# Turning the hidden rows of a feed-forward round by VectorE blocks and an exchange through device memory, in place of TensorE transposes

## The chip, the cores and the metric

The kernel runs on one core of one Trainium2 chip. The metric is the time of one execution in microseconds, the median over repeated runs. The unchanged kernel takes 1331.05 us (three runs, 1330.53 to 1331.22).

## What is computed

A first block of two layers (feed-forward, attention and retention mixer, feed-forward, each with a layer norm) is followed by a second block of two mixer layers. There are 256 tokens and a model width of 1024, all in float32. The change touches the four feed-forward stages alone (feed-forward 1 and 2 of both layers):

```
D_FF = ((8 * D_MODEL // 3 + 127) // 128) * 128        # 2816

def swiglu_ffn(x, w_gu, w_down):
    a, u = jnp.split(x @ w_gu, 2, axis=-1)
    return (jax.nn.silu(a) * u) @ w_down

x = layer_norm(DEEPNORM_ALPHA * x + 0.5 * swiglu_ffn(x, ffn1_w_gu[l], ffn1_w_down[l]), ln1_g[l], ln1_b[l])
```

## The kernel before

The program is one list of jobs, `JOBS`, which all engines walk in the same order; each engine takes from a job the part that is its own. The list thus sets the order on every engine's queue. For a feed-forward stage `ffn_jobs` writes it. Semaphore values (`at[...]`) are counted once over the whole list.

**Precision.** Every product of float32 matrices is made of three passes: each operand is split into a high part (ScalarE copies it to the type fp32r) and a low part (VectorE subtracts the high part from the original). TensorE then multiplies high by high, high by low and low by high into the same PSUM bank (`three`, L818 to L820).

**Weights.** Five slots of 1 MB each hold weight units. SyncE (SP) loads a unit, in two halves, as soon as TensorE has given back the slot (L803, after the wait of L785). ScalarE makes `w_hi` (L1141, waits for the DMA), VectorE makes `w_lo` in place of the raw weights (L1317, waits for ScalarE), TensorE waits for `w_lo`. `with_splits` places these split jobs (`hi`, `lo`) in the list, most of a round ahead of their use.

**A feed-forward stage** has 11 rounds of 256 hidden columns. Round `r` is:

- `gu`: for each of the two token tiles `i`, 24 matmuls of 512 columns (gate and up side by side) into PSUM bank 4 + `i`. ScalarE takes the silu of the gate half (L1182), VectorE multiplies it by 0.5 and the up half (L1404), which gives `hidden`, 128 tokens x 256 columns for each tile.
- `ht`: four TensorE transposes of 128x128 (`turn`, L902) put the hidden rows as columns into PSUM bank 6; ScalarE copies the high part to `lat_hi` (L1190), VectorE the low part to `lat_lo` (L1328, from PSUM).
- `down`: for each token tile 12 matmuls of 512 columns with `lat_hi` and `lat_lo` as the weights of the array, added into banks 0 to 3. `down(r)` stands about two rounds behind `gu(r)`.

In between stand jobs that compute the modulation row of the second block, one chunk a round: `modsum` (VectorE, L1415 and L1417, on a chunk that GpSimd's queue loads), `modsplit` (ScalarE L1186, VectorE L1423), `spread` (one TensorE matmul with one column of weights, L946, that sums over the partitions) and `modrow` (VectorE L1428 and L1429). In the list `ht(r-1)` stands behind `gu(r, 0)`, that is behind the first token tile of the next round, with `spread` right behind it.

ScalarE issues no DMA in this kernel: SP issues the weights, GpSimd the parameters.

## Time and profile before

| what | value |
|---|---|
| median of three runs | 1331.05 us (1330.53 to 1331.22) |
| profiled execution, first to last instruction (its span) | 1328.9 us |
| TensorE (PE) busy | 1311.6 us, 99% |
| VectorE (DVE) busy | 1019.8 us, 77% |
| ScalarE (ACT) busy | 675.3 us, 51% |
| GpSimd (POOL) busy | 105.4 us, 8% |
| DMA | 264.92 MB, 199 GB/s over the span |

For the profiled execution the profile gives the span alone; the median lies 2.15 us above it, which is what a run holds ahead of the first and behind the last instruction, plus the difference between executions. Matmuls are pipelined, so that a matmul's busy time overlaps that of the next one: what a matmul costs is read from the start of one to the start of the next, not from its mean.

### The profile page before, as it was taken

Reading aid. Unit: us, or ns where it says so; the run is one execution under the profiler, and the core shown is the slowest. Engines: PE = TensorE matmul, PEld = TensorE weight load, DVE = VectorE, ACT = ScalarE, POOL = GpSimd, SP = SyncE. Lnnn points to the kernel's source line nnn. Section 1 sums busy time; section 2 is a strip of 40 time slices with the busy share of each in tenths; the row PEclk is TensorE's granted clock in tenths of the full one; section 3 lists DMA queues with packets and bytes.
Section 4 is the critical chain, followed back from the end, with each engine's and each line's share of the span. In section 5 each row is a group of like instructions: output and inputs, shape, how many; then the busy total and the mean of one; then the engine's idle time right before and its main releaser. Section 6 shows DMA issues by size and latency. Waiting matters only on the chain.

```text
span 1328.9 us, 18838 instructions
## 1 busy us (share of the span) xinstructions
PE 1311.6 (99%) x7096; PEld 1110.0 (84%) x7096; DVE 1019.8 (77%) x1625; ACT 675.3 (51%) x1069; POOL 105.4 (8%) x153
## 2 busy tenths in 40 slices
PE   9999999999999999999999999999999999999997
PEld 7888888788888888888887888888889998798995
DVE  6677778887777677777787887778676798966986
ACT  6444444644444344444446545444436667457672
POOL 1010100011011001111010011111000000000000
PEclk9999999999999999999999999999999999999999
DMA  8977756527767656776646358777646473463630
GB/s 268 326 232 229 226 187 208 142 96 246 244 228 233 222 185 219 223 236 228 236 161 202 102 173 292 231 253 235 221 142 200 146 237 129 143 214 118 203 128 32
DMA packets 195049, 264.92 MB, mean 199 GB/s; under 512 B 17232, under 2 KB 140240, under 8 KB 194448
## 3 DMA queue, kind: packets, MB, share of 16 engines
q1 hardware_dynamic: 183248, 223.12, 52.1%
q0 software_dynamic: 11712, 40.60, 8.9%
q8 instruction: 57, 0.93, 0.3%
q14 instruction: 32, 0.26, 0.1%
HBM read 262.61 MB, written 1.07 MB: 198 GB/s over the span
## 4 chain that ended last, share of the span: by engine, by line
PE 87%; DVE 7%; DMA 4%; ACT 1%; issue 1%; SPq 0%; DVEq 0%; ACTq 0%
PE ps L818 26%; PE ps L820 26%; PE ps L819 26%; PE ps L902 4%; DVE w_lo L1317 2%; DMA w_raw<-in_ffn_w_gu 2%; PE ps L1049 2%; DMA w_raw<-in_w_in 1%; PE ps L1084 1%; PE ps L1110 1%; DVE few_first L1346 1%; ACT w_hi L1141 1%; DVE y L1345 1%; PE ps L1018 0%; PE ps L1096 0%
## 5 line engine op out<-in xcount | busy, mean ns | idle before, releaser
L1317 DVE TENSOR_TENSOR w_lo<-w_raw,w_hi 128x1024 fp32r<-128x1024 f32 (+2 forms) x420 | 496.9, 1213 | 128.5 <-ACT w_hi L1141 126.5
L1141 ACT ACTIVATE w_hi<-w_raw 128x1024 fp32r<-128x1024 f32 (+2 forms) x420 | 431.0, 1053 | 247.9 <-DMA w_raw<-in_ffn_w_gu 122.0
L818 PE MATMUL ps<-w_hi,col_hi 128*128 128x512 f32 (+2 forms) x1024 | 396.7, 387 | 3.6 <-DVE w_lo L1324 1.4
L820 PE MATMUL ps<-w_hi,col_lo 128*128 128x512 f32 (+2 forms) x1024 | 392.0, 383 | 0.0
L819 PE MATMUL ps<-w_lo,col_hi 128*128 128x512 f32 (+2 forms) x1024 | 391.9, 383 | 0.0
L818 PEld LDWEIGHTS ps<-w_hi,col_hi 128*128 128x128 f32 x1024 | 192.6, 188 | 44.0 <-DVE w_lo L1317 4.3
L820 PEld LDWEIGHTS ps<-w_hi,col_lo 128*128 128x128 f32 x1024 | 192.5, 188 | 38.2
L819 PEld LDWEIGHTS ps<-w_lo,col_hi 128*128 128x128 f32 x1024 | 192.5, 188 | 34.6
L818 PE MATMUL ps<-w_hi,lat_hi 128*128 128x512 f32 (+2 forms) x544 | 208.8, 384 | 0.0
L820 PE MATMUL ps<-w_hi,lat_lo 128*128 128x512 f32 (+2 forms) x544 | 206.5, 380 | 0.0
L819 PE MATMUL ps<-w_lo,lat_hi 128*128 128x512 f32 (+2 forms) x544 | 206.3, 379 | 0.0
L1182 ACT ACTIVATE arena<-ps 128x256 f32<-128x256 f32 x88 | 33.7, 383 | 201.0 <-PE ps L820 200.8
L818 PEld LDWEIGHTS ps<-w_hi,lat_hi 128*128 128x128 f32 x544 | 102.1, 188 | 19.5 <-ACT arena L1218 1.0
L820 PEld LDWEIGHTS ps<-w_hi,lat_lo 128*128 128x128 f32 x544 | 102.1, 188 | 19.0
L819 PEld LDWEIGHTS ps<-w_lo,lat_hi 128*128 128x128 f32 x544 | 102.2, 188 | 18.3
L818 PE MATMUL ps<-col_hi,w_hi 128*128 128x256 f32 x352 | 101.1, 287 | 0.0
L1417 DVE SCALAR_TENSOR_TENSOR mod<-mod,small 128x192 f32<-128x192 f32 x224 | 93.8, 419 | 8.0
L819 PE MATMUL ps<-col_lo,w_hi 128*128 128x256 f32 x352 | 99.6, 283 | 0.0
L820 PE MATMUL ps<-col_hi,w_lo 128*128 128x256 f32 x352 | 99.6, 283 | 0.0
L1404 DVE SCALAR_TENSOR_TENSOR arena<-arena,ps 128x256 f32<-128x256 f32 x88 | 36.6, 416 | 63.4 <-PE ps L902 49.7
L818 PEld LDWEIGHTS ps<-col_hi,w_hi 128*128 128x128 f32 x352 | 67.4, 192 | 1.2 <-issue 0.7
L819 PEld LDWEIGHTS ps<-col_lo,w_hi 128*128 128x128 f32 x352 | 67.4, 192 | 0.2
(148 smaller groups left out, 1172.8 us busy)
## 6 DMA issues: line engine op xcount, KB each, us to landing
w_raw<-in_ffn_w_gu SPq DMA_DIRECT2D x352, 256.0 KB, 4.5
w_raw<-in_w_in SPq DMA_DIRECT2D x108, 512.0 KB, 4.6
w_raw<-in_ffn_w_down SPq DMA_DIRECT2D x88, 512.0 KB, 4.9
mod<-in_w_ada POOLq DMA_DIRECT2D x32, 768.0 KB, 7.6
w_raw<-in_w_out SPq DMA_DIRECT2D x24, 512.0 KB, 4.5
norm_g<-in_ln_g POOLq DMA_DIRECT2D x8, 512.0 KB, 4.2
norm_b<-in_ln_b POOLq DMA_DIRECT2D x8, 512.0 KB, 6.1
w_raw<-in_w_out SPq DMA_DIRECT2D x16, 256.0 KB, 4.5
```

The lines of the kernel that those rows point to most:

```text
L818: pe.matmul(dst, a_hi, b_hi, start=start, stop=False)
L819: pe.matmul(dst, a_hi, b_lo, start=False, stop=False)
L820: return pe.matmul(dst, a_lo, b_hi, start=False, stop=stop)
L902: last = pe.transpose(ps[0:width, 6 + b, c:c + P], src, ident[:, :])
L1049: last = pe.matmul(ps[:, half, q * keys:(q + 1) * keys], a, b, start=True, stop=True)
L1084: last = pe.matmul(ps[64 * half:64 * half + 64, 2 + i, pair * P:(pair + 1) * P], rows2[:, k, v:v + HD], prob_t[:, half, c:c + P], start=k ...
L1110: last = pe.matmul(ps[:, 2 + i, h * HD:(h + 1) * HD], decayed[:, q, half, pair, :], rows1[:, k, VR + h * HD:VR + (h + 1) * HD], start=q < ...
L1141: act.activation(half_of(w_hi[j], n, h), half_of(raw[j], n, h), ACT.Copy).then_inc(hi_ready, 1)
L1182: act.activation(silu_rows[:, nth % 2, :], ps[:, gu_bank(s, r, i), 0:FU], ACT.Silu)\
L1317: tt(half_of(w_lo[j], n, h), half_of(raw[j], n, h), half_of(w_hi[j], n, h).bitcast(F32), ALU.subtract)\
L1404: stt(hidden[:, r % 2, i, :], silu_rows[:, nth % 2, :], 0.5, ps[:, gu_bank(s, r, i), FU:2 * FU], ALU.mult, ALU.mult).then_inc(hidden_done, 1)
L1417: last = stt(ada_sum, ada_w[:, k, :], c_silu[:, k:k + 1], ada_sum, ALU.mult, ALU.add)
```

## The change

In rounds 1 to 8 of each feed-forward stage (32 rounds in all) the job `ht` is gone. Rounds 0, 9 and 10 keep it. Four jobs stand in its place:

- `hturn` (VectorE, right behind `gu(r, 1)`): one block transpose of `hidden`, 128 partitions x 512 elements, each 32x32 block turned within its group of 32 partitions, into `h_blocks` (in `arena`).
- `hstore` (ScalarE's queue, inside `gu(r+1, 0)`): waits for the block turn, then issues one DMA of 256 KB from `h_blocks` to an internal tensor in device memory.
- `hmove` (ScalarE's queue, inside `gu(r+1, 1)`): waits for the landing of that store, then issues four DMAs of 64 KB that read the blocks back, each into a group of 32 partitions of `h_cols`, in runs of 512 bytes.
- `hparts` (behind `gu(r+2, 0)`): waits for the four landings; ScalarE makes `lat_hi` in two copies of 256 elements, VectorE makes `lat_lo` in two subtractions of 256, now from SBUF. `down(r)` waits for these.

`hidden` of round `r+2` no longer waits for the TensorE transposes but for the block turn. The places of the weight splits are unchanged.

```diff
+ROWS_BY_PE = (0, 9, 10)
...
+    by_pe = lambda r: [("ht", s, r)] if r in ROWS_BY_PE else []
+    blocks, stored, moved, parts = (
+        lambda r, kind=kind: [(kind, s, r)] if r >= 0 and r not in ROWS_BY_PE else [] for kind in ("hturn", "hstore", "hmove", "hparts"))
...
+        jobs += gu(1, 0)[:1] + by_pe(0) + gu(1, 0)[1:] + [("params", s)] + gu(1, 1) + blocks(1)
...
-        jobs += gu(r, 0) + [("ht", s, r - 1)]
+        jobs += gu(r, 0)[:1] + stored(r - 1) + gu(r, 0)[1:] + by_pe(r - 1) + parts(r - 2)
...
-        jobs += gu(r, 1)
+        jobs += gu(r, 1)[:1] + moved(r - 1) + gu(r, 1)[1:] + blocks(r)
...
+    jobs += parts(ROUNDS - 2) + down(tail[0], 0) + down(tail[1], 0) + by_pe(ROUNDS - 1) + down(tail[2], 0) + down(tail[3], 0)
...
+        h_blocks = arena[:, 1536:2560].rearrange("p (r b n) -> p r b n", r=2, b=4)
+        h_cols = arena[:, 2560:3584].rearrange("p (r a n) -> p r a n", r=2, a=4)
...
+        h_stage = nc.dram_tensor("hidden_blocks", (2, 4, 32, 4, P), F32, kind="Internal").ap()
...
+        def h_part(tile, q):
+            return tile[:, q:q + 2, :].rearrange("p g (i a t) -> p g i a t", i=TT, a=4)
+
+        h_as_columns = h_cols.rearrange("p r a (i g t) -> p r g i a t", i=TT, g=2)
...
-                    turns_done(("ht", s, r))
+                    if r in ROWS_BY_PE:
+                        turns_done(("ht", s, r))
+                    else:
+                        pe.wait_ge(h_split, at["hparts", (s, r)])
...
+                elif kind == "hstore":
+                    r = job[2]
+                    nth = at["hturn", (s, r)]
+                    act.wait_ge(h_turned, nth)
+                    if nth > 2:
+                        act.wait_ge(h_moved, 64 * (nth - 2))
+                    act.sem_inc(a_marks, 1)
+                    act.dma_start(h_stage[r % 2].rearrange("a f b n -> (a f) b n"), h_blocks[:, r % 2, :, :]).then_inc(h_stored, 16)
+                elif kind == "hmove":
+                    r = job[2]
+                    nth = at["hturn", (s, r)]
+                    act.wait_ge(h_stored, 16 * nth)
+                    if nth > 2:
+                        act.wait_ge(h_split, nth - 2)
+                    act.sem_inc(a_marks, 1)
+                    for b in range(4):
+                        act.dma_start(h_cols[32 * b:32 * b + 32, r % 2, :, :], h_stage[r % 2, :, :, b, :].rearrange("a f n -> f a n"))\
+                            .then_inc(h_moved, 16)
+                elif kind == "hparts":
+                    r = job[2]
+                    q = 2 * (r % 4)
+                    act.wait_ge(h_moved, at["hmove", (s, r)])
+                    if r >= 4:
+                        act.wait_ge(used, NUMBER[s, ("down", r - 4)] + 1)
+                    act.activation(h_part(lat_hi, q)[:, 0], h_as_columns[:, r % 2, 0], ACT.Copy)
+                    act.activation(h_part(lat_hi, q)[:, 1], h_as_columns[:, r % 2, 1], ACT.Copy).then_inc(hi_part, 1)
...
-                    if r >= 2:
+                    if r >= 2 and r - 2 in ROWS_BY_PE:
                         b, n = TURN["ht", s, r - 2][0]
                         dve.wait_ge(turned[b], n + 1)
+                    elif r >= 2:
+                        dve.wait_ge(h_turned, at["hturn", (s, r - 2)])
...
+                elif kind == "hturn":
+                    r = job[2]
+                    dve.wait_ge(hidden_done, at["hidden", (s, r, 1)])
+                    if at["hturn", (s, r)] > 2:
+                        dve.wait_ge(h_stored, 16 * (at["hturn", (s, r)] - 2))
+                    dve.transpose(h_blocks[:, r % 2, :, :].rearrange("p b (c t) -> p b c t", t=32),
+                                  hidden[:, r % 2, :, :].rearrange("p i (g b f) -> p b (i g) f", g=2, b=4)).then_inc(h_turned, 1)
+                elif kind == "hparts":
+                    r = job[2]
+                    q = 2 * (r % 4)
+                    dve.wait_ge(hi_part, at["hi_part", job])
+                    tt(h_part(lat_lo, q)[:, 0], h_as_columns[:, r % 2, 0], h_part(lat_hi, q)[:, 0].bitcast(F32), ALU.subtract)
+                    tt(h_part(lat_lo, q)[:, 1], h_as_columns[:, r % 2, 1], h_part(lat_hi, q)[:, 1].bitcast(F32), ALU.subtract)\
+                        .then_inc(h_split, 1)
```

What moves on TensorE, at the first spread of the first feed-forward stage (names: `w_hi_61` and `w_lo_60` are a weight slot, `arena` holds `hidden`, `col_hi` the turned activations). Before:

```order
L818 MATMUL ps<-w_hi_61,col_hi 128x512
L819 MATMUL ps<-w_lo_60,col_hi 128x512
L820 MATMUL ps<-w_hi_61,col_lo 128x512
L902 MATMUL ps<-ident,arena 128x128 [waits free0,hidden_done]
L902 MATMUL ps<-ident,arena 128x128 x3
L946 MATMUL ps<-ada_both,ones 1x384 [waits free1,mod_lo]
L818 MATMUL ps<-w_hi_58,col_hi 128x512 [waits hidden_done]
```

And in the changed kernel, at the same place (L836 to L838 are the former L818 to L820, L964 the former L946):

```order
L836 MATMUL ps<-w_hi_61,col_hi 128x512
L837 MATMUL ps<-w_lo_60,col_hi 128x512
L838 MATMUL ps<-w_hi_61,col_lo 128x512
L964 MATMUL ps<-ada_both,ones 1x384 [waits free1,mod_lo]
L836 MATMUL ps<-w_hi_58,col_hi 128x512 [waits hidden_done]
```

The four transposes are gone; the spread matmul follows the weights' matmuls directly, and nothing else moved.

What stands on ScalarE's queue in one steady round of the first stage. Before (L1141 are weight splits, L1182 the silu, L1190 the high part of the turned rows, L1186 `modsplit`):

```order
L1182 ACTIVATE arena<-ps 128x256 [waits hidden_done,group_done]
L1190 ACTIVATE lat_hi<-ps 128x512 [waits turned0]
L1141 ACTIVATE w_hi_64<-w_raw_62 128x1024 [waits w_landed40]
L1141 ACTIVATE w_hi_64<-w_raw_62 128x1024 [waits w_landed41]
L1182 ACTIVATE arena<-ps 128x256 [waits hidden_done,w_used]
L1141 ACTIVATE w_hi_52<-w_raw_50 128x2x512 [waits w_landed00]
L1141 ACTIVATE w_hi_52<-w_raw_50 128x2x512 [waits w_landed01]
L1186 ACTIVATE ada_both<-mod 128x192 [waits mod_summed]
L1141 ACTIVATE w_hi_55<-w_raw_53 128x1024 [waits w_landed10]
L1141 ACTIVATE w_hi_55<-w_raw_53 128x1024 [waits w_landed11]
```

In the changed kernel, from the second of the two high-part copies on (L1238; L1203 is the silu, L1162 the weight splits, L1229 the reads of `hmove`, L1207 `modsplit`, L1220 the store of `hstore`):

```order
L1238 ACTIVATE lat_hi<-arena 128x256
L1162 ACTIVATE w_hi_64<-w_raw_62 128x1024 [waits w_landed40]
L1162 ACTIVATE w_hi_64<-w_raw_62 128x1024 [waits w_landed41]
L1229 DMA arena<-hidden_blocks 32x4x128 [waits hidden_blocks_stored,hidden_split]
L1229 DMA arena<-hidden_blocks 32x4x128 x3
L1203 ACTIVATE arena<-ps 128x256 [waits hidden_done,w_used]
L1162 ACTIVATE w_hi_52<-w_raw_50 128x2x512 [waits w_landed00]
L1162 ACTIVATE w_hi_52<-w_raw_50 128x2x512 [waits w_landed01]
L1207 ACTIVATE ada_both<-mod 128x192 [waits mod_summed]
L1162 ACTIVATE w_hi_55<-w_raw_53 128x1024 [waits w_landed10]
L1162 ACTIVATE w_hi_55<-w_raw_53 128x1024 [waits w_landed11]
L1220 DMA hidden_blocks<-arena 128x512 [waits hidden_blocks_turned,hidden_blocks_moved]
```

Five DMA issues a round are new on this queue. Those of `hmove`, with the wait for the store, stand between the splits of one weight unit and the silu of the second token tile; the store stands behind the last pair of weight splits shown and ahead of the silu of the next round's first token tile.

## Rows read from the trace of the kernel before

**Rows 1.** The page: span, busy time by engine.
```profile
span 1328.9 us, 18838 instructions
PE 1311.6 (99%) x7096; PEld 1110.0 (84%) x7096; DVE 1019.8 (77%) x1625; ACT 675.3 (51%) x1069; POOL 105.4 (8%) x153
```

**Rows 2.** Busy time by stretch: us, engines, clock, DMA share, GB/s.
```profile
34.00:51.00 17.00, 17.00 (x79) 14.05 (x78) 7.13 (x13) 7.59 (x10) 0.00 (x0) 1.00 1.03 384
...
585.00:602.00 17.00, 17.00 (x79) 14.10 (x78) 12.56 (x21) 7.50 (x11) 1.92 (x3) 1.00 0.69 224
```

**Rows 3.** Timeline of PE, transposes without a spread: start, us, engine, line.
```profile
523.42 0.39 PE L820 MATMUL ps<-w_hi,col_lo 128*128 128x512 f32 x1
523.65 0.60 PE L902 MATMUL ps<-ident,arena 128*128 128x128 f32 x4
524.00 0.48 PE L818 MATMUL ps<-w_hi,col_hi 128*128 128x512 f32 x1
524.32 0.39 PE L819 MATMUL ps<-w_lo,col_hi 128*128 128x512 f32 x1
```

**Rows 4.** Timeline of PE, transposes with a spread behind them.
```profile
653.42 0.39 PE L820 MATMUL ps<-w_hi,col_lo 128*128 128x512 f32 x1
...
654.49 0.39 PE L819 MATMUL ps<-w_lo,col_hi 128*128 128x512 f32 x1
...
660.17 0.39 PE L820 MATMUL ps<-w_hi,lat_lo 128*128 128x512 f32 x1
```

**Rows 5.** Timeline of ACT over a steady round; in brackets idle time before.
```profile
572.82 1.06 ACT L1141 ACTIVATE w_hi<-w_raw 128x1024 fp32r<-128x1024 f32 x1 [3.24 <-DMA w_raw<-in_ffn_w_gu]
574.54 0.38 ACT L1182 ACTIVATE arena<-ps 128x256 f32<-128x256 f32 x1 [0.66 <-PE ps L820]
...
575.47 2.00 ACT L1141 ACTIVATE w_hi<-w_raw 128x1024 fp32r<-128x1024 f32 x2
580.60 0.39 ACT L1182 ACTIVATE arena<-ps 128x256 f32<-128x256 f32 x1 [3.13 <-PE ps L820]
...
591.49 0.38 ACT L1182 ACTIVATE arena<-ps 128x256 f32<-128x256 f32 x1 [1.16 <-PE ps L820]
```

**Rows 6.** Timeline of DVE, from the low part of the turned rows on.
```profile
592.55 0.69 DVE L1328 TENSOR_TENSOR lat_lo<-ps,lat_hi 128x512 fp32r<-128x512 f32 x1 [0.15 <-ACT lat_hi L1190]
...
597.43 2.35 DVE L1317 TENSOR_TENSOR w_lo<-w_raw,w_hi 128x1024 fp32r<-128x1024 f32 x2
```

**Rows 7.** Timeline of PE: the first matmul of a down job.
```profile
597.36 0.39 PE L818 MATMUL ps<-w_hi,lat_hi 128*128 128x512 f32 x1
```

**Rows 8.** Groups by line and form of DVE: count, busy us, mean ns.
```profile
L1379 DVE TENSOR_TENSOR arena<-arena 128x256 f32<-128x256 f32 x8 | 3.4, 426 | 0.3
...
L1549 DVE TENSOR_TENSOR arena<-y 128x512 f32<-128x512 f32 x4 | 2.8, 692 | 0.1
```

**Rows 9.** Groups by line and form of ACT.
```profile
L1190 ACT ACTIVATE lat_hi<-ps 128x512 fp32r<-128x512 f32 x44 | 26.2, 595 | 10.4 <-PE ps L902 9.0
...
L1306 ACT ACTIVATE lat_hi<-y 128x256 fp32r<-128x256 f32 x4 | 1.7, 420 | 3.5 <-DVE y L1649 3.5
```

**Rows 10.** Line L803: DMA issues on SP, min/median/max ns, and landing.
```profile
L803 SPq DMA_DIRECT2D w_raw<-in_ffn_w_gu x344: 367/469/1414, 8.6 to 928.6; - x172
...
DMA to landing us min/median/max: 2.4/4.5/12.6
```

**Rows 11.** DMA: queue with packets, MB, share; the kernel's store of 256 KB.
```profile
q1 hardware_dynamic: 183248, 223.12, 52.1%
...
out<-x SPq DMA_DIRECT2D x4, 256.0 KB, 2.1
```

**Rows 12.** Chain that ended last, in the first stage: start, us, what.
```profile
31.53 12.62 DMA w_raw<-in_ffn_w_gu
...
55.38 0.28 DVE ada_both L1423
55.70 0.33 PE ps L946
```

More of the change, by code:

```diff
@@ L169, in ffn_jobs @@
         jobs += gu(0, 1)[:1] + first((6, 7)) + [("xt", s, 1, 1)] + gu(0, 0)[1:] + gu(0, 1)[1:]
-        jobs += gu(1, 0)[:1] + [("ht", s, 0)] + gu(1, 0)[1:] + [("params", s)] + gu(1, 1)
+        jobs += gu(1, 0)[:1] + by_pe(0) + gu(1, 0)[1:] + [("params", s)] + gu(1, 1) + blocks(1)
     else:
@@ L173, in ffn_jobs @@
         jobs += gu(1, 0)[1:] + gu(0, 1) + [("params", s)]
-        jobs += gu(1, 1)[:1] + [("ht", s, 0)] + gu(1, 1)[1:]
+        jobs += gu(1, 1)[:1] + by_pe(0) + gu(1, 1)[1:] + blocks(1)
     lag = 0
     for r in range(2, ROUNDS):
-        jobs += gu(r, 0) + [("ht", s, r - 1)]
+        jobs += gu(r, 0)[:1] + stored(r - 1) + gu(r, 0)[1:] + by_pe(r - 1) + parts(r - 2)
         if r > 2:
@@ L194, in ffn_jobs @@
     tail = list(range(ROUNDS - TAIL, ROUNDS))
-    jobs += down(tail[0], 0) + down(tail[1], 0) + [("ht", s, ROUNDS - 1)] + down(tail[2], 0) + down(tail[3], 0)
+    jobs += parts(ROUNDS - 2) + down(tail[0], 0) + down(tail[1], 0) + by_pe(ROUNDS - 1) + down(tail[2], 0) + down(tail[3], 0)
     jobs += [("norm", s, 0)]
@@ L453, in count_jobs @@
                     ENDS["sums", s, tile] = ENDS[group]
-        if kind in ("xt", "ht", "trlat", "ycols"):
+        if kind in ("xt", "ht", "hparts", "trlat", "ycols"):
             COUNT.add("hi_part", job)
+        if kind in ("hturn", "hparts"):
+            COUNT.add(kind, job[1:])
+        if kind == "hmove":
+            COUNT.add(kind, job[1:], 4 * 16)
         if kind == "ycols" and not TURN[job]:
@@ L710, in build @@
          weighed, y_cols, ret_mixed, half_sum, var_ready, rstd_ready, h_ready, x_ready, y_ready, rope_done, rotated, idx_w_ready,
-         idx_summed, rope_a_done, rope_k_done, squares, latent, folded, mod_summed, mod_hi, mod_lo, mod_row) = (
+         idx_summed, rope_a_done, rope_k_done, squares, latent, folded, mod_summed, mod_hi, mod_lo, mod_row,
+         h_turned, h_moved, h_split, h_stored) = (
             sem(n) for n in ("group_done", "silu_done", "hidden_done", "copied", "hi_part", "scores", "score_free", "maxed",
@@ L714, in build @@
                              "h_ready", "x_ready", "y_ready", "rope_done", "rotated", "idx_w_ready", "idx_summed",
-                             "rope_a_done", "rope_k_done", "squares", "latent", "folded", "mod_summed", "mod_hi", "mod_lo", "mod_row"))
+                             "rope_a_done", "rope_k_done", "squares", "latent", "folded", "mod_summed", "mod_hi", "mod_lo", "mod_row",
+                             "hidden_blocks_turned", "hidden_blocks_moved", "hidden_split", "hidden_blocks_stored"))
         x_in = [[sem(f"x_landed{i}{h}") for h in range(2)] for i in range(TT)]
@@ L723, in build @@
         const_ready, c_ready, out_landed = sem("const_ready"), sem("c_ready"), sem("out_landed")
-        v_steps, g_steps, v_marks, g_marks, s_marks = (
-            sem(n) for n in ("vector_steps", "gpsimd_steps", "vector_marks", "gpsimd_marks", "sync_marks"))
+        v_steps, g_steps, v_marks, g_marks, s_marks, a_marks = (
+            sem(n) for n in ("vector_steps", "gpsimd_steps", "vector_marks", "gpsimd_marks", "sync_marks", "scalar_marks"))
         ends = {"used": used, "group_done": group_done}
```

## The prediction

> **What bounds the kernel now.** I read the page first: over a span of 1328.9 us TensorE is busy for 1311.6 us, VectorE for 77% and ScalarE for 51% [rows 1]. A busy share of 99% of pipelined matmuls could still hide slack, so I looked at the starts. In a steady round the weights' matmuls of 512 columns start (660.17 - 654.49) / 25 = 0.227 us apart [rows 4], without a gap. A round is 16.95 us long (574.54 to 591.49) [rows 5], and its 72 matmuls of that kind fill 72 x 0.227 = 16.3 us of it. The rest, 0.6 us, is the transposes and the spread. The stretch table says the same: TensorE busy for 17.00 of 17.00 us at a granted clock of 1.00, with VectorE at 12.56, ScalarE at 7.50 and the DMA engines at 0.69 [rows 2]. So in the feed-forward rounds TensorE's own queue sets the pace, and what leaves this queue leaves the time, as long as nobody else becomes late. One place differs: in the first stage a weight half took 12.62 us to land, and the chain from there to 55.70 us runs over ScalarE and VectorE until the spread matmul, which waited for them [rows 12]. DMA was full there: share 1.03 in that stretch [rows 2].
>
> **What is removed from TensorE.** 32 rounds x 4 transposes. Their busy time of 0.60 us for four [rows 3] is not their price, for it overlaps the next matmul. From start to start the four take 524.00 - 523.65 = 0.35 us, and the first weights' matmul behind them holds the next one back: 524.32 - 523.42 = 0.90 us against 2 x 0.227 us, so 0.45 us in all [rows 3]. With a spread behind them, transposes and spread together cost 654.49 - 653.42 = 1.07 less 0.45, that is 0.62 us [rows 4]. How this splits once the spread stands alone no row shows. I take 0.35 us for the transposes, the start-to-start time; 0.45 us is the upper end, and 0.26 us (0.35 less the 0.09 us of hold-up, which the spread might then pay) the lower. In each stage one of the eight turns has no spread (round 1) and seven have one. The sum is 4 x 0.45 + 28 x 0.35 = **11.6 us**, with ends of 4 x 0.45 + 28 x 0.26 = 9.1 and 32 x 0.45 = 14.4 us.
>
> A transpose thus costs about 0.09 us of TensorE here. The Trainium skill, page "VectorE: DVE Perf Modes", section "The three transpose paths", gives 390 ns for one 128x128 transpose on TensorE (of bf16). By that figure the sum would be 128 x 0.39 = 50 us. The trace disagrees by a factor of four, because here four of them run in a pipeline.
>
> **What is added on VectorE.** The block turn of 128x512 has no row in this kernel. From below, an operation of 256 elements takes 0.43 us; the nearest row is the 128x512 subtraction with both operands in SBUF, 0.69 us [rows 8]; from above I take twice the nearest, 1.4 us. I use 0.69. The low part is now two subtractions of 256, 2 x 0.43 = 0.86 us, in place of one of 0.69 [rows 6, 8]. So VectorE has 0.69 + 0.17 = 0.86 us more a round: 12.56 + 0.86 = 13.4 of 16.6 us. That is covered. The same section of the Trainium skill gives 311 ns for 128x128 on VectorE; four of those would be an estimated 1.24 us, inside my bounds, and no run here shows it yet.
>
> **What is added on ScalarE.** Two copies of 256 from SBUF, 2 x 0.42, for one of 0.60 [rows 9]: +0.24 us. Five DMA issues, at 0.37 to 0.47 us each as on SP [rows 10]: +2.35 us at most. Busy plus issuing becomes 7.50 + 0.24 + 2.35 = 10.1 of 16.6 us. The new waits matter more, since all of ScalarE's work queues behind them. The store goes out when the split that began at 572.82 ends, at 573.9. By then the block turn is long done: it follows the silu of the round before, which in the next round stands at 580.60, ten microseconds ahead of the next store. The four reads are due behind the pair that ends at 575.47 + 2.00, with the extra copies at 577.7 [rows 5]. So the store has 3.8 us to land. The kernel's own store of 256 KB landed in 2.1 us, weight loads of the same size in 4.5 us (median) [rows 10, 11]. At 4.5 us ScalarE is held for 0.7 us, then issues for 1.9 us, and is free at 580.3; the silu behind it waits for TensorE until 580.60 anyway [rows 5]. So I cost it at nothing; the 3.13 us of idle time ahead of that silu is the cover. Without it, `hidden` and the weight splits would slip.
>
> **Who waits for the new chain.** `down(r)` now waits for `hparts`. The low part ended at 592.55 + 0.69 = 593.24 [rows 6] and `down` began at 597.36 [rows 7]: 4.1 us of slack against 0.4 us of longer copies and subtractions. The four reads have most of a round to land. The pair of weight splits that VectorE starts at 597.43 [rows 6] is used after both `down` jobs (24 x 0.227 = 5.4 us) and the first half of a `gu` (2.7 us), from 605.5 on, and ends at 599.8: 5.7 us of slack against 0.9 us of more work.
>
> **DMA.** Each round adds 128 packets of 2 KB and 512 of 512 bytes. By packets, at 0.521 x 16 x 1328.9 / 183248 = 60 ns each [rows 11], that is 640 x 60 / 16 = 2.4 us of all 16 engines; by bytes (0.52 MB at 223 MB in 692 us) 1.6 us. The share rises from 0.69 to about 0.8 to 0.85. Weights land some 2 us later at worst, which the slack above covers.
>
> **The first stage.** There the spread at 55.70 waits for VectorE [rows 12]. What TensorE saves ahead of it, the turns of rounds 1 and 2 (0.45 + 0.35 = 0.8 us), goes into this wait. VectorE's own chain keeps its length: a low part of 0.69 us leaves it and a block turn of about 0.69 enters. The store of round 1 goes into the full DMA queues and may hold the late weight half back by 128 x 60 / 16 = 0.5 to 0.8 us; I take 0.6.
>
> **Sum.** 11.6 - 0.8 - 0.6 = 10.2 us less. Of the profiled execution this makes a span of 1318.7. The median of the runs stands 2.15 us above the profiled span, and the change does not touch what lies around it: 1331.05 - 10.2 = **1320.8 us**. The mixer stages hold none of the four jobs and move as a whole.
>
> **Rivals.**
> 1. *The transfers make weights late.* For: share 1.03 in the first stage, a landing of 12.6 us. Against: SP waits for TensorE's slots, not for DMA, in the steady rounds. If the first stage loses its whole gain (0.45 + 7 x 0.35 = 2.9 us) and one round's traffic (2.4 us) on top, 11.6 - 2.9 - 2.4 = 6.3 remain: 1324.8 us.
> 2. *ScalarE is held by the store (slower).* `hmove` waits in ScalarE's queue for the landing in device memory. Room a round is 16.6 - 10.1 = 6.5 us, so it decides from a landing of 3.8 + 6.5 = 10.3 us on. At the 12.6 us that a transfer took in the first stage [rows 10, 12] ScalarE's round is 10.1 + 8.8 = 18.9 us, 1.95 over the present one. In the eight rounds of one stage that is +15.6; less the 8.7 us that the other three gain, 1338.0 us. If it held in all 32, +62 us. The Trainium skill, page "DMA: Bandwidth & Descriptors", section "Anatomy of one DMA — SWDGE (gpsimd) path", says that most of a DMA's fixed 2 us is the wait for the write's receipt, and that it can be surprisingly long when device memory is the target. The 2.1 us of [rows 11] speak against a long one, though those stores ran alone at the end.
> 3. *Nothing comes of it.* If every round's saving reappears as a wait for `hidden_split` or for weights, as in the first stage: 1331.
>
> **Chances.** Forecast (savings of 8 to 14 us) 0.65, rival 1 0.17, rival 3 0.05, rival 2 (with a block turn of several us as its sibling) 0.13. A difference of over 0.2% is 2.7 us, about what a measurement can tell. Faster is then 0.65 + 0.17 = 0.82, same 0.05, slower 0.13. The range takes in the ends of the transposes' price on one side and rival 1 with some more on the other: 1317.5 to 1327.5.
>
> **What would show it.** Right: the round 16.6 us long (16.95 before), the span near 1318.7, 128 transposes fewer, TensorE still at 17.00 of 17.00; ScalarE's wait for the store under 1 us in steady rounds; the block turn near 0.7 us. Wrong: idle time of TensorE with `hidden_split` or `w_lo` as its releaser, a store landing of over 10 us, issues on ScalarE of over 1 us each, a block turn of over 3.9 us (then VectorE's 12.7 us and the turn fill the round), or a spread that costs the same 0.62 us alone.

## The result and the profile after

| | changed | before |
|---|---|---|
| median | 1319.41 us (1318.00 to 1319.70, 4 runs) | 1331.13 us (1330.53 to 1331.33, 4 runs) |
| ratio | 0.9911, 95% interval 0.9899 to 0.9924 | |
| profiled execution | 1319.7 us, span 1317.9 us | span 1328.9 us |

The change takes 11.7 us off, 0.89%. The forecast was 10.2 us off, 1320.8 us.

The page of the changed kernel, span and busy time by engine, the store's and the reads' queue, and the DMA issues with the median us to landing:

```profile
span 1317.9 us, 18920 instructions
...
PE 1298.7 (99%) x6968; PEld 1095.1 (83%) x6968; DVE 1044.3 (79%) x1689; ACT 679.9 (52%) x1101; POOL 105.7 (8%) x153
...
q10 hardware_dynamic: 23040, 16.79, 4.0%
...
w_raw<-in_ffn_w_gu SPq DMA_DIRECT2D x352, 256.0 KB, 4.9
...
hidden_blocks<-arena ACTq DMA_DIRECT2D x32, 256.0 KB, 5.7
arena<-hidden_blocks ACTq DMA_DIRECT2D x128, 64.0 KB, 4.2
```

Against [rows 1], TensorE has 128 instructions fewer (7096 to 6968) and is 12.9 us less busy, close to what the span lost (11.0 us). VectorE gained 24.5 us and ScalarE 4.6 us of work, without cost in most places. Gate and up weights land in 4.9 us (median) where it was 4.5 [rows 10].

Busy time by stretch (us, engines PE, PEld, DVE, ACT, POOL, granted clock, DMA share, GB/s):

```profile
51.00:68.00 17.00, 15.27 (x67) 12.05 (x66) 16.50 (x27) 10.43 (x16) 2.70 (x4) 1.00 0.92 306
...
585.00:602.00 17.00, 17.00 (x77) 13.96 (x76) 13.82 (x23) 8.47 (x14) 1.93 (x3) 1.00 0.85 265
```

Beside [rows 2], the steady stretch (the last row) still shows TensorE without a gap at a clock of 1.00, VectorE 1.3 us and ScalarE 1.0 us fuller, and the DMA share at 0.85 where it was 0.69. The first row is of the first stage, the one place where TensorE stood idle for long within the rounds.

**Where a round's gain comes from.** Timeline of PE in the changed kernel, at a spread (start, us, engine, line):

```profile
584.12 0.39 PE L838 MATMUL ps<-w_hi,col_lo 128*128 128x512 f32 x1
584.35 0.34 PE L964 MATMUL ps<-ada_both,ones 128*1 128x384 f32 x1
584.53 0.40 PE L836 MATMUL ps<-w_hi,col_hi 128*128 128x512 f32 x1
584.77 0.39 PE L837 MATMUL ps<-w_lo,col_hi 128*128 128x512 f32 x1
```

From the last weights' matmul ahead of it to the second one behind it the spread takes 584.77 - 584.12 = 0.65 us; less 2 x 0.227 us, its own price is 0.20 us. Transposes and spread together cost 0.62 us [rows 4]. So the transposes ahead of a spread were worth 0.42 us, not the 0.35 us of the forecast. Every other spread that nothing held up gives the same: 0.19 us in the changed kernel (27 of its 28 without transposes), 0.62 us with transposes before (31 of 32). The distance of two silus says the same. Timeline of ACT in the changed kernel over one steady round (in brackets the idle time before, and what ended it; ACTq are issues):

```profile
568.01 0.38 ACT L1203 ACTIVATE arena<-ps 128x256 f32<-128x256 f32 x1 [3.67 <-PE ps L838]
...
579.90 0.34 ACTq L1220 DMA_DIRECT2D hidden_blocks<-arena  x1
584.55 0.38 ACT L1203 ACTIVATE arena<-ps 128x256 f32<-128x256 f32 x1 [3.69 <-PE ps L838]
...
585.82 1.06 ACT L1162 ACTIVATE w_hi<-w_raw 128x1024 fp32r<-128x1024 f32 x1 [0.28 <-DMA w_raw<-in_ffn_w_gu]
587.64 1.06 ACT L1162 ACTIVATE w_hi<-w_raw 128x1024 fp32r<-128x1024 f32 x1 [0.76 <-DMA w_raw<-in_ffn_w_gu]
587.74 1.79 ACTq L1229 DMA_DIRECT2D arena<-hidden_blocks  x4
590.20 0.38 ACT L1203 ACTIVATE arena<-ps 128x256 f32<-128x256 f32 x1 [1.50 <-PE ps L838]
```

A round is 584.55 - 568.01 = 16.54 us, where it was 16.95 us [rows 5]: 0.41 us less. The reads were issued 7.8 us after the store in this round. Over the 32 rounds it was 3.3 to 13.1 us, 6.1 in the median, against landings of 3.2 to 8.0 us, 5.7 in the median. In 8 rounds the reads went out 0.1 us behind the landing, so they had waited for it; ScalarE was still at the weight split ahead of them and lost nothing by it. Both silus still wait for TensorE, the second with 1.50 us to spare (3.13 before).

**Where the gain is lost.** What ScalarE's silu waited for in the changed kernel (us in total, times, longest us):

```profile
ACT arena L1203 <- PE ps L838: 197.0, 81, 5.1
...
ACT arena L1203 <- issue: 3.1, 2, 2.0
```

and what TensorE waited for at the spread:

```profile
PE ps L964 <- DVE ada_both L1486: 1.7, 1, 1.7
```

The silu never waited for a landing in device memory: among its releasers is no DMA, and issuing held it twice in the whole run. TensorE never waited for `lat_lo` from the exchange. Its one long wait within the rounds is the spread of the first stage. The chain that ended last there, in the changed kernel (start, us, what):

```profile
31.80 13.31 DMA w_raw<-in_ffn_w_gu
...
53.50 0.71 DVE arena L1460
...
56.45 0.28 DVE ada_both L1486
...
56.78 0.33 PE ps L964
```

Against [rows 12] the spread comes 1.08 us later (56.78, was 55.70). The weight half took 13.31 us instead of 12.62 and landed at 45.11 instead of 44.15, 0.96 us later. The block turn of 0.71 us (L1460) is new in the chain, but from the landing to the spread the chain takes 11.67 us where it took 11.55, because the low part of the turned rows left it. That is this line of the chain before:

```profile
46.41 0.68 DVE lat_lo L1328
```

In the second profiled execution of the same kernel (below) the chain ran over a neighbouring half that landed at 47.65 and over the issuing of the four reads, 2.55 us of ScalarE behind it; the spread started at 56.62. The two chains are nearly tied.

Stage by stage, from the first silu to the last, the profiled executions give:

| kernel | stage 1 | stage 2 | stage 3 | stage 4 | sum |
|---|---|---|---|---|---|
| before | 156.3 | 160.4 | 160.1 | 159.4 | 636.2 |
| changed | 154.6 | 156.9 | 156.7 | 157.2 | 625.4 |

Stages 2 and 3 gain 3.5 and 3.4 us; 0.45 + 7 x 0.42 makes 3.4. The first gains 1.7 and the fourth 2.2. The rest of the program takes 692.5 us instead of 692.7.

### The profile page after: what moved, and what is told of

It reads as the page before. It is cut to its first block, busy times and chain, and to the rows that moved or that the text cites. A ratio compares the mean times of both kernels' runs of the same rounds, so it can differ in the third digit from the quotient of the medians.

```text
span 1317.9 us, 18920 instructions
## 1 busy us (share of the span) xinstructions
PE 1298.7 (99%) x6968; PEld 1095.1 (83%) x6968; DVE 1044.3 (79%) x1689; ACT 679.9 (52%) x1101; POOL 105.7 (8%) x153
## 4 chain that ended last, share of the span: by engine, by line
PE 88%; DVE 6%; DMA 3%; ACT 1%; issue 1%; SPq 1%; DVEq 0%; ACTq 0%
PE ps L836 27%; PE ps L838 26%; PE ps L837 26%; PE ps L920 3%; DMA w_raw<-in_ffn_w_gu 3%; DVE w_lo L1364 2%; PE ps L1070 2%; PE ps L1105 1%; PE ps L1131 1%; DMA w_raw<-in_w_in 1%; DVE few_first L1393 1%; DVE y L1392 1%; PE ps L1039 0%; PE ps L1117 0%; ACT w_hi L1162 0%
## 5 line engine op out<-in xcount | busy, mean ns | idle before, releaser
L1162 ACT ACTIVATE w_hi<-w_raw 128x1024 fp32r<-128x1024 f32 (+2 forms) x420 | 432.5, 1053 | 233.7 <-DMA w_raw<-in_ffn_w_gu 94.0
L836 PE MATMUL ps<-w_hi,col_hi 128*128 128x512 f32 (+2 forms) x1024 | 396.9, 388 | 3.9 <-DVE w_lo L1364 2.1
L838 PE MATMUL ps<-w_hi,col_lo 128*128 128x512 f32 (+2 forms) x1024 | 392.0, 383 | 0.0
L836 PEld LDWEIGHTS ps<-w_hi,col_hi 128*128 128x128 f32 x1024 | 192.5, 188 | 47.8 <-DVE w_lo L1364 4.1
L838 PEld LDWEIGHTS ps<-w_hi,col_lo 128*128 128x128 f32 x1024 | 192.4, 188 | 38.6
L836 PE MATMUL ps<-w_hi,lat_hi 128*128 128x512 f32 (+2 forms) x544 | 208.8, 384 | 0.0
L838 PE MATMUL ps<-w_hi,lat_lo 128*128 128x512 f32 (+2 forms) x544 | 206.5, 380 | 0.0
L1203 ACT ACTIVATE arena<-ps 128x256 f32<-128x256 f32 x88 | 33.7, 383 | 200.0 <-PE ps L838 197.0
L836 PEld LDWEIGHTS ps<-w_hi,lat_hi 128*128 128x128 f32 x544 | 102.1, 188 | 19.5 <-issue 0.7
L838 PEld LDWEIGHTS ps<-w_hi,lat_lo 128*128 128x128 f32 x544 | 102.1, 188 | 19.0
L836 PE MATMUL ps<-col_hi,w_hi 128*128 128x256 f32 x352 | 101.1, 287 | 0.0
L838 PE MATMUL ps<-col_hi,w_lo 128*128 128x256 f32 x352 | 99.6, 283 | 0.0
L836 PEld LDWEIGHTS ps<-col_hi,w_hi 128*128 128x128 f32 x352 | 67.4, 191 | 1.2 <-issue 0.7
```

The source lines that it names most:

```text
L836: pe.matmul(dst, a_hi, b_hi, start=start, stop=False)
L838: return pe.matmul(dst, a_lo, b_hi, start=False, stop=stop)
L1162: act.activation(half_of(w_hi[j], n, h), half_of(raw[j], n, h), ACT.Copy).then_inc(hi_ready, 1)
L1203: act.activation(silu_rows[:, nth % 2, :], ps[:, gu_bank(s, r, i), 0:FU], ACT.Silu)\
```

## The experiments

Where lines of these kernels are named, they are a few numbers higher than in the changed kernel (L970 is the spread L964, L1466 the block turn L1460, L842 the weights' matmul L836). The block turn is L1459 in the kernel with the additions alone and L1442 in the one without the exchange; L1381 and L1374 are the low part of what TensorE turned. "Now" is the median of the run, "before" that of the kernel before on the same chip in the same series; chips differ by some tenths, so the series differ too.

### Which rounds TensorE should keep

```diff
+def rows_by_pe(s):
+    return (0, 1, 2, 9, 10) if s == 0 else ROWS_BY_PE
...
-    by_pe = lambda r: [("ht", s, r)] if r in ROWS_BY_PE else []
+    by_pe = lambda r: [("ht", s, r)] if r in rows_by_pe(s) else []
```

and the other uses of `ROWS_BY_PE` alike; the two buffers of a turn are then told apart by the number of the turn, not of the round.

> As the changed kernel, but in the first feed-forward stage TensorE keeps the turns of rounds 1 and 2 too (rounds 0, 1, 2, 9 and 10); the other three stages as changed. Theory (the first stage's chain of one weight load, module sum and low halves sets its spread of round 2, and both the block turn of 0.71 us and the late weight of the first round lie in it): the spread starts 1.1 us earlier than in the changed kernel (at about 55.7 us as before, against 56.8), nothing is lost elsewhere, and the time is 1318.3 us. Rival (the first stage's loss is made by transfers in general, not by these two rounds): the spread stays within 0.3 us of 56.8 and the time is 1319.4. Rival (the turns that TensorE takes back are work of its own and nothing waited for them): 1319.4 + 2 x 0.62 = 1320.6.

The second kernel has `(0, 1, 9, 10) if s == 0`:

> As the changed kernel, but in the first stage TensorE keeps round 1's turn (rounds 0, 1, 9 and 10); round 2 is turned by VectorE. Theory: the weight that lands late is helped, the block turn of round 2 stays in the chain: the spread starts about 0.4 us earlier than in the changed kernel (56.4 against 56.8), time 1319.0 us. Rival (the whole 1.1 us comes from the late weight): spread at 55.7, 1318.3. Rival (the whole comes from the block turn): spread at 56.8, 1319.4.

The third has `(0, 10)` in all stages:

> As the changed kernel, but round 9 is turned by VectorE too in all four stages; TensorE keeps rounds 0 and 10. Theory (each turned round frees TensorE of its transposes, 0.41 us by the distance of two rounds, as long as nothing waits for the moved tile): 4 x 0.41 = 1.7 us less, 1317.7 us. Rival (at the stage's end the store's landing of up to 8 us isn't covered, since the reads come one round later and the last rounds are short of other work): the wait eats it in each stage, 1319.4 to 1323.

The fourth has `(0, 1, 2, 10) if s == 0 else (0, 10)`:

> Both edits: in the first stage TensorE keeps rounds 0, 1, 2 and 10, in the other three rounds 0 and 10. Theory: the two gains add, since they lie at different ends of a stage: 1319.4 - 1.1 - 1.7 = 1316.6 us. Rival (round 9's reads hold ScalarE at the end of a stage): 1318.3 or above.

| kernel | now | before | ratio, 95% interval |
|---|---|---|---|
| rounds 1 and 2 back in stage 1 | 1318.19 us (1318.02 to 1318.62) | 1330.73 | 0.9904, 0.9890 to 0.9919 |
| round 1 back in stage 1 | 1319.49 (1317.79 to 1321.29) | 1330.73 | 0.9914, 0.9899 to 0.9929 |
| round 9 turned too | 1319.70 (1317.93 to 1322.12) | 1330.73 | 0.9916, 0.9902 to 0.9931 |
| both edits | 1317.23 (1316.15 to 1319.87) | 1330.73 | 0.9901, 0.9884 to 0.9917 |

These medians lie closer together than the runs of one kernel scatter, so here the traces decide. The chain of the first kernel in the first stage:

```profile
31.89 12.40 DMA w_raw<-in_ffn_w_gu
...
46.55 0.69 DVE lat_lo L1381
...
55.84 0.33 PE ps L970
```

With both turns back on TensorE the block turn is out of the chain and the low part back in it, the weight half lands in 12.40 us, and the spread starts at 55.84: 0.94 us earlier than in the changed kernel. TensorE's two turns cost nothing, since they lie in its wait. The chain with round 1 alone given back:

```profile
31.69 12.07 DMA w_raw<-in_ffn_w_gu
...
46.02 0.68 DVE lat_lo L1381
...
52.74 0.71 DVE arena L1466
...
56.02 0.33 PE ps L970
```

The block turn is still in it (0.71 us) and the spread starts at 56.02, which is earlier than the 56.4 expected, because the weight half took 1.24 us less than in the changed kernel (12.07 against 13.31). These chains tell the two causes apart when they are counted from the landing to the spread: 11.55 us before and with both turns given back (low part alone in it), 11.67 us in the changed kernel (block turn alone), 12.26 us here (low part of round 1 and block turn of round 2). The block turn in the low part's place thus costs the chain 0.12 us, and the late weight is the rest: 0.82 of the 0.94 us that the first of these kernels gets back. The 0.4 us that I expected from giving back round 1 alone left out that its low part returns to the chain.

Giving round 9 to VectorE missed its 1317.7 us; the median lies in the range of the rival. In the trace, though, it shortens each stage. The stages of that kernel take 154.4, 156.0, 156.2 and 155.6 us, 622.2 in sum: 3.2 us less than the changed kernel, of which the four turns explain 4 x 0.41 = 1.6. But the rest of the program takes 695.1 us instead of 692.5 in that execution, and the median shows no gain. The waits behind the stages differ from one execution to the next by that much, so this run alone settles nothing on round 9.

Therefore the changed kernel and the two best went once more, on one chip and in one series:

> The changed kernel as it is, on one chip with the next two, since the runs of the narrower first stage so far stood beside the kernel before alone. Expected 1319.4 us, within 0.6.

> The kernel whose first stage leaves rounds 1 and 2 to TensorE, again. Theory (the 1.1 us of the first stage come back whole): 1.1 us under the changed kernel of this same series. Rival (what the first stage gets back is lost again in the mixers behind): within 0.4 us of it.

> The kernel with both edits, again. Theory (the second edit's 1.7 us are TensorE's, but of a stage's end, where its profiles so far showed the mixers behind taking half a us more each): 0.7 to 1.2 us under the kernel of the first edit, 1.8 to 2.3 under the changed kernel. Rival (the two edits add in full): 2.8 us under the changed kernel. Rival (the second edit is worth nothing): equal to the kernel of the first edit.

| kernel | now | before | ratio, 95% interval |
|---|---|---|---|
| changed | 1319.92 (1318.98 to 1320.89) | 1331.59 | 0.9916, 0.9902 to 0.9929 |
| rounds 1 and 2 back in stage 1 | 1318.69 (1317.56 to 1320.06) | 1331.59 | 0.9906, 0.9892 to 0.9919 |
| both edits | 1317.40 (1316.59 to 1323.08) | 1331.59 | 0.9907, 0.9891 to 0.9924 |

The medians fall by 1.23 and again by 1.29 us; in the other series the second step was 0.96 us. The first step is that of its theory (1.1). The second is a little above its own (0.7 to 1.2, and 2.5 against 1.8 to 2.3 under the changed kernel). The intervals overlap, and so do the single runs. The ratios, which go by all runs, show no second step here (0.9906 and 0.9907), for one run of the last kernel stood at 1323.08. So the first edit's gain is likely and the second's is open: the version with both has the lowest median in both series, 2.5 us under the changed one, and no more than that is shown.

The first step is not the first stage alone. In both pairs of profiled executions (spans 1317.9 and 1316.5 us, 1317.2 and 1315.8 us) the first stage takes 1.0 us less with rounds 1 and 2 given back, the fourth 0.9 us less, and the rest 0.5 us more.

### The change in one stage

```diff
+def rows_by_pe(s):
+    return ROWS_BY_PE if s == 3 else tuple(range(11))
```

> The change in the fourth feed-forward stage alone; the first three as before the change. Theory (each of stages two to four gains by TensorE's removed transposes, round by round, 8 to 9 x 0.41 us): 1331.1 - 3.3 = 1327.8 us. Rival (gain depends on what one stage hands on to the next, so that one stage alone loses its gain in the mixer behind it): 1329.5 or above.

The index `s` counts the mixer stages too, so this was the third feed-forward stage, not the fourth, as its eight block turns from 519 to 631 us show. Now 1327.19 us (1326.39 to 1327.56), before 1331.43, ratio 0.9968 (0.9956 to 0.9981): 4.2 us less where 3.3 was expected, and the interval reaches from 2.5 to 5.9. In the trace the third stage takes 156.9 us and the three others 155.9, 159.8 and 159.6. So the 3.2 us belong to the stage itself, and it keeps them.

### The additions alone

TensorE keeps all turns; block turn, store and reads run beside:

```diff
-    by_pe = lambda r: [("ht", s, r)] if r in ROWS_BY_PE else []
+    by_pe = lambda r: [("ht", s, r)]
...
-                    act.activation(h_part(lat_hi, q)[:, 0], h_as_columns[:, r % 2, 0], ACT.Copy)
-                    act.activation(h_part(lat_hi, q)[:, 1], h_as_columns[:, r % 2, 1], ACT.Copy).then_inc(hi_part, 1)
```

> TensorE keeps every turn and its copies out of PSUM, as before the change; in rounds 1 to 8 of each stage the block turn on VectorE, the store and the four reads run beside, into tiles of their own, and the place where the read tile would be taken waits for the reads alone. So this is the cost of what the change adds, with nothing taken away. Theory (what is added lies in slack of VectorE, ScalarE and the queues, except in the first stage): before plus about 1 us, 1332.2 us. Rival (the additions cost in every round, and hide in the changed kernel behind what was freed): 0.2 us per round x 32, 1337.5.

Now 1332.96 us (1332.49 to 1333.88, 11 runs), before 1331.43 (16 runs), ratio 1.0012 (1.0003 to 1.0020): 1.5 us more. The trace puts it in the first stage, which takes 158.0 us instead of 156.3; the other three take 159.9, 160.1 and 159.8 (before 160.4, 160.1, 159.4). Its chain in the first stage:

```profile
31.78 13.53 DMA w_raw<-in_ffn_w_gu
...
47.57 0.68 DVE lat_lo L1374
...
54.29 0.71 DVE arena L1459
...
57.57 0.33 PE ps L970
```

The late weight (13.53 us) is as in the changed kernel. But both the low part and the block turn lie in this chain, which takes 12.26 us from landing to spread, 0.6 us more than in the changed kernel. In the rounds that lie clear of it what is added costs nothing that can be seen. The 11.7 us of the change and these 1.5 us together make 13.2 us of gross saving, near the 4 x 0.45 + 28 x 0.42 = 13.6 from the rows. The agreement is loose: the intervals allow 1.7 us on the first number and 1.1 us on the second, these 1.5 us hold the 0.6 us of longer chain, and what the change loses in the fourth stage is not in them. Stages 2 and 3, with 3.5 and 3.4 us each, are the firmer one.

### The exchange left out, and doubled

The first kernel leaves the exchange of blocks out of the computation; the split reads the block-turned tile:

```diff
-        h_as_columns = h_cols.rearrange("p r a (i g t) -> p r g i a t", i=TT, g=2)
+        h_as_columns = h_blocks.rearrange("p r a (i g t) -> p r g i a t", i=TT, g=2)
...
-                    act.dma_start(h_stage[r % 2].rearrange("a f b n -> (a f) b n"), h_blocks[:, r % 2, :, :]).then_inc(h_stored, 16)
```

> As the changed kernel without the store and the reads: the split takes its rows from the block-turned tile as it is, so the exchange of blocks is left out of the computation and the block turn stays. Theory (the exchange's transfers are hidden but for the first stage's late weight): 1319.4 - 0.4 to 1 us, 1318.4 to 1319.0. Rival (store and reads cost issue time on ScalarE or a share of the transfers in every round, 32 x 0.1 us or more): 1316 or below.

The second issues all of it twice:

```diff
+                    act.dma_start(h_again[r % 2].rearrange("a f b n -> (a f) b n"), h_blocks[:, r % 2, :, :]).then_inc(h_stored, 16)
...
+                    for b in range(4):
+                        act.dma_start(h_spare[32 * b:32 * b + 32, r % 2, :, :], h_again[r % 2, :, :, b, :].rearrange("a f n -> f a n"))\
+                            .then_inc(h_moved, 16)
```

> As the changed kernel, with the store and the four reads issued twice, the second set to memory and a tile that nobody reads, on the same queue. Theory (hidden by slack: ScalarE has some 8 us of a round of 16.5 free, the transfers' share goes from 0.85 to about 0.95): 1 to 2 us over the changed kernel, mostly in the first stage, 1320.4 to 1321.4. Rival (transfers are at their edge, and weights come late in every stage): 1325 or more.

Without the exchange 1319.24 us (1317.56 to 1319.85), ratio 0.9907 (0.9893 to 0.9920); doubled 1321.36 (1320.10 to 1323.39), ratio 0.9927 (0.9915 to 0.9939); before 1331.43 in both. The first lies 0.2 us above its theory and far from its rival, the second in its theory. So 16.8 MB through device memory, once, cost within what can be told from nothing. The second time costs 2.1 us by the ratios (0.9927 against 0.9911, with overlapping intervals). It doesn't fall mostly in the first stage, as expected: in the profiled execution (1323.39 us, the slowest of the five) that stage takes 155.8 us, 1.2 more than in the changed kernel, and the fourth 160.3, 3.1 more; in each of them TensorE waits 1.7 us at a spread. Stages 2 and 3 lose 0.2 us at most, though their steady stretch shows that the transfers are near the edge. Doubled exchange, by stretch:

```profile
585.00:602.00 17.00, 17.00 (x77) 13.97 (x76) 14.36 (x23) 7.79 (x11) 1.93 (x3) 1.00 0.99 315
```

A DMA share of 0.99, and TensorE still busy for all of it; its gate and up weights land in 5.7 us.

The two kernels also size the late weight. In the first stage the weight half at the head of the chain took 12.62 us before, 12.07, 12.40 and 12.58 us in three kernels that don't store round 1 there, and 12.31 without any exchange; with one store of round 1 it took 13.31 (changed), 13.42 (round 9 turned too) and 13.53 us (additions alone), and with two 14.10. Where other pieces headed the chain the same half took 12.15 to 12.27 us without a store of round 1 (three kernels), and 13.11 (the changed kernel again) and 13.55 us with one. One store of 256 KB thus makes it 0.5 to 1.5 us later, by the nearest and the farthest pair. Without the exchange the chain is:

```profile
31.95 12.31 DMA w_raw<-in_ffn_w_gu
...
52.65 0.71 DVE arena L1442
...
55.92 0.34 PE ps L964
```

Landing at 44.26 instead of 45.11, spread at 55.92 instead of 56.78: 0.85 and 0.86 us. What the store delays, it delays the spread by.

This kernel also speaks against the exchange as the cause of the fourth stage's loss. Its stage took 157.7 us, the changed kernel's 157.2, and both opened late: in the changed kernel the chain there runs over a weight half (776.41, 5.52 us to land), ScalarE's split of it and the layer norm on VectorE. The fourth stage took 156.3 and 156.1 us in the two executions with rounds 1 and 2 given back, and 156.8 and 157.8 with both edits. Two executions of one kernel thus differ by 1.0 us, so chance may explain it. But both executions of the changed kernel (157.2 and 157.0) stand 0.9 us above those with rounds 1 and 2 given back, whose fourth stage is the same program. What decides it was not found.

### The cover taken away

The reads stand directly behind the store on ScalarE's queue:

```diff
-        jobs += gu(r, 0)[:1] + stored(r - 1) + gu(r, 0)[1:] + by_pe(r - 1) + parts(r - 2)
+        jobs += gu(r, 0)[:1] + stored(r - 1) + moved(r - 1) + gu(r, 0)[1:] + by_pe(r - 1) + parts(r - 2)
...
-        jobs += gu(r, 1)[:1] + moved(r - 1) + gu(r, 1)[1:] + blocks(r)
+        jobs += gu(r, 1) + blocks(r)
```

> As the changed kernel, but the four reads of a round's block stand directly behind its store on ScalarE's queue, so nothing covers the store's landing (median 5.7 us in the changed kernel's profile) and ScalarE is held for it. Theory (ScalarE is busy about 8.5 us of a round of 16.54 and issues for some 2.2 us, so 8.5 + 2.2 + 5.7 = 16.4 us still just fit, but its evictions and silu come late by up to the landing where TensorE waits for them): somewhat slower than the changed kernel, 1322 to 1340. Rival (cover doesn't matter, a DMA that waits doesn't hold the engine behind it): 1319.4, unchanged. Rival (ScalarE becomes the bound in each round and each landing goes into the round): 32 rounds x 3 to 5 us, 1415 or more.

Now 1376.51 us (1368.27 to 1383.96), before 1331.32, ratio 1.0322 (1.0263 to 1.0380): 57 us above the changed kernel. None of the ranges held it: the cover is worth far more than I had thought, and far less than a whole landing in each round. Timeline of ACT in one round:

```profile
434.50 0.34 ACTq L1220 DMA_DIRECT2D hidden_blocks<-arena  x1
443.12 1.97 ACTq L1229 DMA_DIRECT2D arena<-hidden_blocks  x4
445.20 0.38 ACT L1203 ACTIVATE arena<-ps 128x256 f32<-128x256 f32 x1 [11.02 <-issue]
```

and of PE at the same place:

```profile
443.32 0.39 PE L838 MATMUL ps<-w_hi,col_lo 128*128 128x512 f32 x1
447.13 0.77 PE L836 MATMUL ps<-w_hi,lat_hi 128*128 128x512 f32 x1 [3.43 <-DVE lat_lo L1467]
447.70 0.63 PE L837 MATMUL ps<-w_lo,lat_hi 128*128 128x512 f32 x1
```

ScalarE issued nothing for 8.6 us between store and reads, the second longest of the 32 waits (4.0 to 9.1 us, 6.2 in the median). Silu, high part and low part came late, and `down` waited. The Trainium skill, page "DMA: Bandwidth & Descriptors", section "Anatomy of one DMA — SWDGE (gpsimd) path", says that a semaphore's wait happens on the issuing sequencer, ahead of the dispatch. The trace agrees: the 11.02 us of idle time ahead of the silu are put down to issuing and none of them to TensorE, so the silu stood behind the wait. The largest waits of the run, of ACT and of PE:

```profile
ACT arena L1203 <- issue: 150.7, 16, 11.4
...
ACT arena L1203 <- DMA arena<-hidden_blocks: 131.0, 16, 9.3
```

```profile
PE ps L836 <- DVE lat_lo L1467: 28.8, 18, 3.4
```

In all 32 rounds ScalarE stood idle ahead of this silu for the store or its issues, 282 us together, or 8.8 us each, the issuing counted in; in the changed kernel it has 3.7 us of idle time there. My error was to add busy time and landing (16.4 of 16.54 us) as if ScalarE's work could close up around the hole. It can't: its round has fixed places, 3.7 us of idle time ahead of the silu and 1.5 us ahead of the other, and whatever exceeds the gap at the place of the wait arrives late, however idle the engine is elsewhere. TensorE's waits sum to 55.1 us here and 10.9 in the changed kernel, 44.2 more, and its busy time grew by 19.2 us:

```profile
span 1381.1 us, 18920 instructions
...
PE 1317.9 (95%) x6968; PEld 1102.2 (80%) x6968; DVE 1041.1 (75%) x1689; ACT 670.4 (49%) x1101; POOL 105.7 (8%) x153
```

The two make 63.4 us, the growth of the span (63.2). The second of them is mostly the clock, below.

## Why the prediction was right, and where its sizes were off

Time, sign and mechanism came as forecast: 11.7 us less where 10.2 was said, 1319.41 us in a range of 1317.5 to 1327.5. By its own steps:

- **What is removed.** The sum of 11.6 us was too small. The term that was off is 28 turns with a spread at 0.35 us; they measured 0.62 - 0.20 = 0.42. The spread alone did not pay the hold-up that I left with it. The gross saving is 4 x 0.45 + 28 x 0.42 = 13.6 us, and the kernel with the additions alone gives 13.2 from the other side, roughly. One transpose in a row of four thus costs TensorE about 0.1 us. By the 390 ns (128x128 of bf16) of the Trainium skill, page "VectorE: DVE Perf Modes", section "The three transpose paths", an estimated 50 us would have come out; the trace disagrees.
- **VectorE.** The block turn took 0.711 us in all 32 cases; 0.69 was taken from the nearest row. By the same section of the Trainium skill (311 ns for 128x128 of bf16) an estimated 1.24 us would have come out for four times 128x128; the trace disagrees, at 0.71 us for 128x512 of float32. The halves of the low part took 0.43 and 0.42 us as forecast.
- **ScalarE.** The copies took 0.41 us each. Issues sum to 0.34 + 4 x 0.45 = 2.2 us a round. The 2.35 us that I called the most were no bound, as they took SP's median for one issue: in the first stage the four reads of one round took 2.91 us to issue, and the silu came 2.0 us late by it. The store's landing had a median of 5.7 us, above the 2.1 to 4.5 us expected, and a longest of 8.0. It cost nothing, as the reads came up later than planned, 6.1 us behind the store in the median and not 3.8: the splits ahead of them wait for their own weights. The cost of nothing was right in part by luck, for landing and cover were both larger than I had said, and in 8 of the 32 rounds the reads did wait for the landing.
- **DMA.** Share 0.85, as forecast. Gate and up weights land 0.4 us later by the median.
- **First stage.** The loss was put at 0.8 + 0.6 = 1.4 us; the stage gains 1.7 instead of 3.4, so 1.7 us went. Both mechanisms were named: TensorE's saved turns (0.45 + 0.42 us) went into the wait, and the weight half came late, its landing by 0.85 us against the kernel without the exchange and by 0.96 against the kernel before, rather than 0.6 (0.3 of the 0.96 is a later start of the load). What was off is that term's size. That VectorE's own chain keeps its length was right to 0.12 us.
- **Not foreseen.** The fourth stage's opening lost about 1.2 us. The kernel without an exchange lost as much there. The cause stays open.
- **Rivals.** Rival 1 (late weights) happens in the first stage alone, and to a third of its price. Rival 2 (ScalarE held) is real: with the cover gone the kernel is 57 us slower. The price that I gave for all 32 rounds was 62 us over the kernel before; it measured 45. The way to its threshold was wrong: I added all free time of a round (6.5 us) to the distance of the reads (3.8 us), 10.3 us. With the reads directly behind the store the same way gives 6.5 us, and landings of 6.1 us in the median were enough for 57 us. What counts is the 3.7 us of idle time ahead of the next silu. Only the place of the reads kept it away. Rival 3 did not happen.

In sum: span -13.6 + 1.7 (first stage) + 1.2 (fourth stage's opening) - 0.3 (the rest) = -11.0 us.

## What to carry to other kernels

When one engine bounds a stage without a gap, price what leaves its queue from start to start between its neighbours, once with and once without what stands next to it; here this gave 13.6 us where a guess at the split gave 11.6. A wait for a DMA on an engine that also computes must be set against the free time at the place of the wait, not against the free time of the round: the reads went out some 6 us behind the store in both kernels; with ScalarE's own work in between the exchange was nearly free, and with the reads directly behind the store it cost 57 us. And a change that relieves one engine by loading others should leave out the stretch where those others are the chain: with two of 32 rounds given back to TensorE the spread there started 0.94 us earlier, and the median fell by 1.2 us, likely but within the scatter of the runs.

## What the runs showed of the hardware that I had not expected

**A pause can cost twice.** In the kernel without cover TensorE stood idle for 3.43 us from 443.7 on, and after it the granted clock fell. By stretch (columns as above):

```profile
182.00:184.00 2.00, 2.00 (x6) 1.54 (x6) 2.00 (x5) 1.53 (x2) 0.00 (x0) 0.54 0.00 0
...
444.00:446.00 2.00, 0.00 (x0) 0.00 (x0) 0.30 (x1) 0.80 (x3) 0.00 (x0) 1.00 1.04 376
446.00:448.00 2.00, 0.87 (x2) 0.80 (x3) 1.71 (x6) 2.00 (x4) 0.00 (x0) 0.66 1.13 291
448.00:450.00 2.00, 2.00 (x6) 1.52 (x6) 1.82 (x6) 2.00 (x4) 0.50 (x1) 0.50 1.03 302
450.00:452.00 2.00, 2.00 (x11) 1.65 (x10) 1.93 (x4) 0.95 (x3) 0.00 (x0) 0.98 0.07 21
...
972.00:974.00 2.00, 0.15 (x1) 0.18 (x2) 1.44 (x5) 2.00 (x5) 0.00 (x0) 1.00 0.94 277
974.00:976.00 2.00, 2.00 (x10) 1.62 (x11) 1.75 (x5) 2.00 (x4) 0.50 (x1) 1.00 1.10 347
```

At 0.50, the lower level of 1.2 GHz, six matmuls fall into 2 us instead of eleven. The first two behind the pause start 0.57 us apart (447.13 and 447.70) where 0.227 is usual. Over the run the mean clock was 0.988 against 0.998. On some 1318 us of busy time that is an estimated 13 us, most of the 19.2 us of extra busy time. The four runs of this kernel lie apart the same way: 1368.27, 1370.14, 1382.88 (the profiled one) and 1383.96 us at mean clocks of 0.993, 0.991, 0.988 and 0.986. The changed kernel's pause of 1.7 us in the first stage did not lower it: 1.00 in the stretch from 51 to 68 us.

The length of a pause alone doesn't tell whether the clock falls. In the feed-forward stages of the kernel without cover it fell, for about 4 us each time, behind pauses of 1.98 us (from 177.8 on, the first row), 2.51 (389.2), 3.43, 1.97 (488.4), 2.91 (573.8), 1.93 (689.3) and 1.94 us (997.4). It stayed at 1.00 behind pauses of 2.49 (152.2), 2.56 (629.1), 2.60 (916.3) and 2.95 us (970.9, the last two rows). At the opening of the program, too, it fell behind 1.82 us (7.6) in this kernel, and not behind 2.63 us (6.6) in the kernel with the additions alone. These runs do not show what decides it.

**A store to device memory under load** landed in 5.7 us (median) beside weights of the same size in 4.9 us, where the kernel's own stores at the end took 2.1 us [rows 11]. That points to the load more than to the direction, but no run here has a load of a weight on idle queues beside it. The moment counts too: the same 32 stores landed in 4.0 us (median) in the kernel with the additions alone, whose steady stretch (585 to 602 us) had a DMA share of 0.77 instead of 0.85.
